# Decoder layer with 32 experts: the down-projection weights of experts 2 to 26 are issued from ScalarE's DMA queue instead of SyncE's

## The reference

```python
def clamped_swiglu(hidden):
    glu, lin = hidden[..., ::2], hidden[..., 1::2]
    glu = jnp.minimum(glu, SWIGLU_LIMIT)
    lin = jnp.clip(lin, -SWIGLU_LIMIT, SWIGLU_LIMIT)
    return glu * jax.nn.sigmoid(SWIGLU_ALPHA * glu) * (lin + 1.0)

def moe_ffn(h, w_router, b_router, w_mlp1, b_mlp1, w_mlp2, b_mlp2):
    ...
    for e in range(N_EXPERTS):
        hid = clamped_swiglu(xt @ w_mlp1[e] + b_mlp1[e])
        y = y + combine[:, e:e + 1] * (hid @ w_mlp2[e] + b_mlp2[e])
    return y.reshape(B, S, D)
```

## Time and profile before

| | before |
|---|---|
| median of 3 executions | 1136.12 us (1135.59 to 1137.19) |
| the profiled execution's own time | 1137.09 us |
| its span (first to last instruction) | 1135.2 us |
| mean granted TensorE clock | 0.99 of full speed |
| TensorE matmuls busy | 1084.9 us, 96% |
| VectorE, ScalarE busy | 322.2 us (28%), 228.6 us (20%) |
| read from HBM | 445.22 MB |
| mean DMA rate over the span | 394 GB/s |

### The profile page before, as it was taken

One profiled execution on the slowest core, in us unless ns is written; L12 is line 12 of the kernel. 1 busy time (PEld: TensorE's weight loads), 2 busy tenths in 40 slices (PEclk: granted clock), 3 DMA queues, 4 the chain that ended last, 5 costly groups with the idle time before them and its releaser, 6 DMA issues.

```text
span 1135.2 us, 15726 instructions
## 1 busy us (share of the span) xinstructions
PE 1084.9 (96%) x6536; PEld 522.0 (46%) x6536; DVE 322.2 (28%) x733; ACT 228.6 (20%) x411; POOL 8.1 (1%) x14
## 2 busy tenths in 40 slices
PE   9999999989999999999999999999999999999996
PEld 6888899843333333343333333333333333334331
DVE  6987775581111111121111111111111111012112
ACT  5667565440000100010010000000000000001001
POOL 0000000000000000000000000000000000000000
PEclk9999999999999999999999999999999999999999
DMA  9866868699999999999999999999999999999996
GB/s 354 295 193 238 289 209 331 230 388 419 436 431 435 432 433 432 435 433 433 432 434 434 432 435 433 433 432 435 433 432 433 434 434 431 431 430 429 432 426 250
DMA packets 41728, 446.74 MB, mean 394 GB/s; under 512 B 4832, under 2 KB 5728, under 8 KB 25088
## 3 DMA queue, kind: packets, MB, share of 16 engines
q1 hardware_dynamic: 41408, 445.76, 94.0%
q10 hardware_dynamic: 288, 0.52, 0.1%
HBM read 445.22 MB, written 1.05 MB: 393 GB/s over the span
## 4 chain that ended last, share of the span: by engine, by line
PE 58%; DMA 35%; SPq 3%; DVE 3%; issue 1%; ACT 0%; DVEq 0%
DMA ring<-in_w_mlp 33%; PE bank L1155 23%; PE bank L1199 9%; PE bank L685 5%; PE bank L687 5%; PE bank L686 5%; PE bank L1057 4%; PE bank L1045 2%; DMA w_raw<-in_w_in 2%; SPq L609 1%; PE bank L1094 1%; SPq L488 1%; SPq L502 1%; PE bank L927 1%; PE bank L911 1%; PE bank L1113 1%
## 5 line engine op out<-in xcount | busy, mean ns | idle before, releaser
L1155 PE MATMUL bank<-ring,live 128*64 128x512 f32 x2048 | 468.2, 605 | 27.9 <-DMA ring<-in_w_mlp 27.7
L1155 PEld LDWEIGHTS bank<-ring,live 128*64 128x64 f32 x2048 | 143.8, 138 | 310.4 <-issue 286.0
L1199 PE MATMUL bank<-ring,live 128*64 128x512 f32 x992 | 220.8, 596 | 6.8 <-DMA ring<-in_w_mlp 6.8
L1919 DVE COPY live<-bank 128x256 f32<-128x256 f32 x32 | 13.6, 425 | 527.8 <-PE bank L1087 527.8
L1199 PEld LDWEIGHTS bank<-ring,live 128*64 128x64 f32 x992 | 70.8, 137 | 130.8 <-issue 122.6
L1517 ACT ACTIVATE live<-bank 128x512 f32<-128x512 f32 x31 | 18.5, 597 | 325.1 <-PE bank L1094 325.1
L1589 DVE TENSOR_TENSOR w_low<-w_raw,w_high 128x1024 fp32r<-128x1024 f32 x61 | 72.3, 1221 | 23.8 <-ACT w_high L1291 23.6
L2009 DVE TENSOR_SCALAR live<-bank 128x256 f32<-128x256 f32 x64 | 24.2, 420 | 193.1 <-PE bank L1155 193.1
L1291 ACT ACTIVATE w_high<-w_raw 128x1024 fp32r<-128x1024 f32 x61 | 63.1, 1059 | 34.7 <-PE bank L687 16.6
L1513 ACT ACTIVATE live<-live 128x512 f32<-128x512 f32 x32 | 20.3, 635 | 239.4 <-DVE live L2009 239.4
L1045 PEld LDWEIGHTS bank<-pick,live 128*128 128x128 bf16 x1488 | 52.0, 118 | 27.0 <-issue 27.0
(11 more groups left out here) (253 smaller groups left out, 859.2 us busy)
## 6 DMA issues: line engine op xcount, KB each, us to landing
ring<-in_w_mlp SPq DMA_DIRECT2D x73, 4096.0 KB, 47.1
ring<-in_w_mlp SPq DMA_DIRECT2D x34, 2048.0 KB, 49.2
ring<-in_w_mlp SPq DMA_DIRECT2D x22, 1024.0 KB, 11.0
w_raw<-in_w_in SPq DMA_DIRECT2D x21, 512.0 KB, 10.0
w_raw<-in_w_mem_kv SPq DMA_DIRECT2D x16, 512.0 KB, 4.9
w_raw<-in_w_mix_out SPq DMA_DIRECT2D x8, 512.0 KB, 5.4
w_raw<-in_w_mem_q SPq DMA_DIRECT2D x8, 512.0 KB, 3.9
w_raw<-in_w_mem_o SPq DMA_DIRECT2D x8, 512.0 KB, 6.0
```

The lines of the kernel that those rows point to most:

```text
L1155: mm = pe.matmul(up[j][64 * g:64 * g + SLOTS, :], x_e[:, k, :], columns(row, j, g), start=False, stop=(k == KC - 1))
L1199: mm = pe.matmul(to[64 * g:64 * g + SLOTS, :], stationary[:, P * c + 64 * u:P * c + 64 * u + SLOTS], slot(at)[:, col:col + 512], start=(u ...
```

## The change

SP no longer issues the down pieces of experts 2 to 26: its loop issues two up pieces for each expert. ACT issues them on its own queue, each right after `copy_result`. The condition stays the same, since `copy_result(n)` waits for `down_done` of stage n, and the piece goes into the place that this stage has used. To know the places by number, ACT's loop over the experts is split: one pass by itself, then 12 rounds of two experts with a load behind each, then 5 passes without a load (`more * E + 5`). Down pieces of experts 27 to 31 stay on SP.

```diff
             load_up_halves(3, 1, 1)
-            load_down(2, 0, 0)
             with sp.Fori(0, E // 2 - 4) as i:
                 for parity in range(2):
                     load_up(sp.snap(2 * i + parity + 4), sp.snap(2 * i + parity + 2), parity)
-                    load_down(sp.snap(2 * i + parity + 3), sp.snap(2 * i + parity + 1), 1 - parity)
...
-            with act.Fori(0, act.snap(more * E + (E - 2))) as i:
-                n, one_ago = act.snap(i + 2), act.snap(i + 1)
+
+            def load_down(e, at):
+                act.dma_start(slot(at), expert_src(e, UPS)).then_inc(piece_in[at], 16)
+
+            def through_expert(n, one_ago):
                 copy_hidden(one_ago, banks[2][:, :], hidT)
                 sigmoids(n)
-                act.wait_ge(gathered, act.snap(i + 3))
+                act.wait_ge(gathered, act.snap(n + 1))
                 take_tokens()
                 act.wait_ge(hid_ready, n)
                 copy_result(one_ago, banks[2][:, :], y_e)
+
+            through_expert(2, 1)
+            load_down(2, UPS)
+            with act.Fori(0, E // 2 - 4) as i:
+                for parity in range(2):
+                    through_expert(act.snap(2 * i + parity + 3), act.snap(2 * i + parity + 2))
+                    load_down(act.snap(2 * i + parity + 3), UPS if parity else 3 + UPS)
+            with act.Fori(0, act.snap(more * E + 5)) as i:
+                through_expert(act.snap(i + E - 5), act.snap(i + E - 6))
```

## The result

The changed kernel is slower: 1140.75 us in the median of 7 executions (1138.03 to 1142.10), against 1135.85 us for the kernel before (7 executions, 1135.12 to 1137.19). The ratio is 1.0038 (+4.3 us), 95% interval 1.0028 to 1.0047, which is +3.2 to +5.3 us; the medians differ by +4.9 us. The forecast size, +8.4 us, was nearly twice the measured one.

A forecast was written before the change was run, and what follows sets the result against it. The prediction took the DMA transfers at 433 GB/s as the bound. A PE lag of 14.7 us plus 1.7 us slow clock, less 8.05 us caught up, gave +8.4 us on 1136.12: 1144.5 us, range 1135.5 to 1149.0.

The forecast's parts named there:

- What bounds the kernel, and what the change leaves alone: Expert part: DMA at 433 GB/s is the bound and stays so; SP's saved and ACT's 25 added issues cost 0.
- The order of landing: Middle experts: down pieces land early, up 1 lands 15.0 us later, PE's waits move there; no throughput cost.
- Equal shares: Two DMA queues: each gets half the rate, so a down piece takes 19.4 us from its issue, not 47.
- The sum of 0: Whole kernel: if several issuing engines save only issue time, already hidden on SP, the change is worth 0.
- the sum at the end: From expert 26's up 1 on: PE's lag plus slow clock, less what it catches up, gives +8.35 us.
- 14.7 + 1.7 us behind at expert 26's up 1: Expert 26's up 1: PE lags its old position by 14.7 us, plus 1.70 us for one slow-clock group.
- my own working: Middle experts, up 1: 10.6 us at half rate puts 0.55 of a second down piece ahead, 15.0 us later landing.
- the lower bound, +5.3 us: End of the expert part: PE's last wait lies one expert earlier, so another 3.04 us is caught up.
- 8.05 us to catch up: From expert 26's up 1 on: PE regains eight waits and 1.70 us of slow clock, 8.05 us in all.
- No change: Whole kernel: pieces land in order of issue, or the shift isn't paid; 1136.1 us, chance 0.14.
- Faster: Expert part: two queues feed the DMA engines better, over 437.3 GB/s; 1123.7 us at 444 GB/s, chance 0.12.
- SP's queue first: Down stage: ACT's pieces move only when SP has nothing open; +31 us, 1167 us; much slower by either way 0.12.

The follow-up runs named there:

- the run with the new loop: Against the changed kernel: ACT's loop kept in its new form, but SP issues all transfers as before; 1135.77 us, ratio 1.0000 to the kernel before.
- the hand-over at 19: Against the changed kernel: ACT issues down pieces only up to expert 18, SP again from 19 on; 1135.33 us, ratio 0.9998 to the kernel before.
- the repeat of the changed kernel: The changed kernel timed and traced again without any edit; 1138.53 us in the median, ratio 1.003 to the kernel before.

## Why the prediction was right in kind and too large

*What bounds the kernel, and what the change leaves alone:* right. The rate is 433 GB/s and the share 1.00 in both. SP's issues saved and ACT's 25 issues of 0.34 us cost nothing, as the run with the new loop and the hand-over at 19 (17 such issues, +0) show.

*The order of landing:* right in kind. The down pieces overtake, the waits move to up 1, all ahead of the down stage vanish, the first comes earlier. Equal shares would give 19.4 us to landing; measured were 19.3 us at the least, 23.2 us in the median and 24.4 us at the most. If the whole time to landing is transfer, ACT's queue gets 9.69 / 23.2 = 0.42 of the rate while its piece is under way; what the start of a transfer takes of the 23.2 us was not measured, so 0.42 is an estimate from below. One sign failed: expert 28's up stage was to start 10 to 14 us later than at 1002.4; it started at 1011.44, 9.0 us later. Of the two rules of the Trainium skill (DMA: Bandwidth & Descriptors) the one on taking turns between queues (Queues, rings and completion order) agrees with the trace roughly, in 0.42 for 0.5. The one that several issuing engines only save issue time (Issuing engines are not separate DMA queues) agrees with the trace for the rate (433 GB/s in both). The sum of 0 that the prediction drew from it does not: measured were +4.9 us, as the order of arrival changed.

*The step that failed is the sum at the end,* "14.7 + 1.7 - 8.05 = +8.35 us". By the first trace it is 3.9 us, and two of its terms were too far off: the lag was put too high and what is caught up too low.

- *14.7 + 1.7 us behind at expert 26's up 1.* Measured 13.8 us in all (969.32 against 955.56), 2.6 us less. I had PE wait there, and behind a slow clock. The waits don't come at each expert: they are 5.4 and some 3 us long, two experts apart in most cases, and in this execution the last fell on expert 25. There the lag was 15.3 us (941.93 against 926.60) and the slow clock cost 1.4 us, near my 14.7 and 1.7. With 23.2 us to landing in place of 19.4, my own working gives 10.6 / 23.2 = 0.46 piece and 13.8 us, so part of this nearness is luck. I named this case as the lower bound, +5.3 us. In the execution where the last long wait fell on expert 26 the lag with its slow clock was 969.58 + 2.87 - 955.56 = 16.9 us, my 16.4.
- *8.05 us to catch up.* Measured 162.15 - 152.3 = 9.8 us, 1.8 us more. I had added the idle times in brackets. A matmul's end in the profile is modelled, so the idle time shown behind it is shorter than what the wait costs. The rows of TensorE in the kernel before show it for one wait:

```profile
1068.65 3.65 PE L1155 MATMUL bank<-ring,live 128*64 128x512 f32 x16
1073.14 3.65 PE L1155 MATMUL bank<-ring,live 128*64 128x512 f32 x16 [0.84 <-DMA ring<-in_w_mlp]
```

From start to start 4.49 us, where 16 such matmuls without a wait take half of the 7.02 us that the chain shows for 32, 3.51 us: 0.98 us lost, with 0.84 us in the bracket. The changed kernel does the same work from 969.32 us on without a wait, so the two timelines can be held against each other group by group. Seven of the eight waits cost 0.06 to 0.23 us each more than their brackets, and the one at 1058.66 us costs 0.41 us more, as the down stage ahead of it took 7.32 us in place of 7.09. With 0.05 us in the slow-clock group and 0.08 us at 1104.47 us, where no bracket stands, this is 1.74 us, the difference to within 0.05 us. The second trace of the old order says the same: 6.1 us in nine brackets, 7.9 us lost.

With 9.8 us in place of 8.05, and the last wait at expert 26, the sum would have been +6.6 us; with the last wait one expert earlier +3.6 us. The measured +4.9 us lies between. The three traces have both cases among them; how the other executions divide is not known.

*The rivals.* "No change" is out by the interval, 1.0028 to 1.0047. "Faster" is out by the rate, 433 and not over 437 GB/s. "SP's queue first" is out by the 23.2 us and the missing waits ahead of the down stage.

*What stays open:* whether the share is 0.42 or nearer 0.5, why the waits mostly fall two experts apart, and how the median divides into lag and what is caught up, since both change from one execution to the next. No run was made for any of these.

## What to carry to other kernels

When a kernel is bound by a saturated transfer queue, as here at 433 GB/s, look at the order of arrival before you add a second queue. No version with a second queue beat the one queue in the order of use. Here the second queue brought forward what was needed later and delayed what was needed now. In the middle this was invisible, since rate and period stayed; it was paid at the end, by the lag less what the consumer could catch up. Handing the transfers back to one queue eight experts earlier (at 19 instead of 27) made it free, two experts earlier nearly so. Sum up a wait's cost from start to start of the work around it, not from the idle time in the row.

## What the runs showed of the hardware that I had not expected

- A 4.19 MB piece on a second queue, beside a queue that is never empty, took 23.1 to 23.3 us in the median to land in all six versions that have it, against 9.69 us at the full rate: an estimate of 0.42 of the rate, if all of that time is transfer.
- Executions of one kernel spread over 6 us; the three with a trace have 432 to 433 GB/s all the same. The first wait of over 5 us comes at expert 11 or 12, the last at 24, 25 or 26, and in these three the end follows from where the last falls.
- The first 32 matmuls behind a wait of 5.3 to 5.4 us took between 8.41 and 10.09 us in place of 7.09: the slow clock costs from 1.3 to 3.0 us behind waits of the same length. In the trace of the first hand-over the granted clock was 0.56 from 649.40 to 652.40 us and then 1.00 (8.41 us); in the repeat of the changed kernel it was 0.50 from 737.30 to 741.00 us, 0.62 to 744.00 us and then 1.00 (10.09 us).
